# Layer 1's gate modulation: products and sums on VectorE instead of matmuls on TensorE

## The reference

```python
sc, scc = silu(c), silu(c_ctx)
for l in range(2):
    shift, scale, gate = split(sc @ w_ada[l] + b_ada[l], 3)        # w_ada[l]: 2048 x 6144
    shift_c, scale_c, gate_c = split(scc @ w_ada[l] + b_ada[l], 3)
    h = rms(x, norm_w[l]) * (1 + scale) + shift
    ...
    x = x + gate * merge_out(o_a, o_b, o_c, z, w_out[l])
    if not last:
        xc = xc + gate_c * merge_out(oa_c, ob_c, oc_c, z_c, w_out[l])
```

## Time and profile before

| | us |
|---|---|
| median of 3 runs | 3337.48 |
| lowest, highest | 3337.32, 3339.63 |
| the profiled execution | 3336.91 |
| its span, first to last instruction | 3335.1 |
| TensorE busy | 3297.0 |
| VectorE busy | 2125.5 |
| ScalarE busy | 1413.5 |
| POOL busy | 596.1 |

### The profile page before, as it was taken

One profiled execution on the slowest core, in us unless ns is written; L12 is line 12 of the kernel. 1 busy time (PEld: TensorE's weight loads), 2 busy tenths in 40 slices (PEclk: granted clock), 3 DMA queues, 4 the chain that ended last, 5 costly groups with the idle time before them and its releaser, 6 DMA issues.

```text
span 3335.1 us, 57286 instructions
## 1 busy us (share of the span) xinstructions
PE 3297.0 (99%) x21136; PEld 2818.5 (85%) x21136; DVE 2125.5 (64%) x3139; ACT 1413.5 (42%) x2160; POOL 596.1 (18%) x531
## 2 busy tenths in 40 slices
PE   8999999999999999999999999999999999999999
PEld 8999999989888888788987787778877788888978
DVE  7887877567776666767664556634553375764665
ACT  5444445544433343454532423532342263544353
POOL 4999920111440000000300000000001100000000
PEclk9999999999999999999999999999999999999999
DMA  6555555564677877777732222121235443422225
GB/s 221 183 179 184 187 185 184 185 211 165 243 266 263 278 264 272 264 260 269 249 101 98 73 88 75 54 82 63 94 108 202 145 152 108 134 94 95 95 96 181
DMA packets 158866, 554.58 MB, mean 166 GB/s; under 512 B 17456, under 2 KB 23728, under 8 KB 158640
## 3 DMA queue, kind: packets, MB, share of 16 engines
q1 hardware_dynamic: 154144, 534.67, 47.3%
q0 software_dynamic: 4496, 16.78, 1.5%
HBM read 545.09 MB, written 6.29 MB: 165 GB/s over the span
## 4 chain that ended last, share of the span: by engine, by line
PE 92%; DVE 4%; ACT 2%; DVEq 1%; issue 1%; DMA 0%; ACTq 0%; POOL 0%; SPq 0%
PE psum L2012 19%; PE psum L2014 18%; PE psum L2013 18%; PE psum L2037 14%; PE psum L2038 7%; PE psum L2066 3%; PE psum L2342 2%; PE psum L2368 2%; PE psum L2353 2%; DVE wlo L1253 1%; PE psum L2138 1%; PE psum L2299 1%; ACT whi L798 0%; PE psum L2228 0%; ACTq L869 0%
## 5 line engine op out<-in xcount | busy, mean ns | idle before, releaser
L1253 DVE TENSOR_TENSOR wlo<-raw,whi 128x1024 fp32r<-128x1024 f32 (+3 forms) x844 | 1033.6, 1230 | 570.0 <-ACT whi L798 541.2
L798 ACT ACTIVATE whi<-raw 128x1024 fp32r<-128x1024 f32 (+3 forms) x844 | 864.9, 1030 | 1058.0 <-PE psum L2014 632.9
L2012 PE MATMUL psum<-hcat,whi 128*128 128x256 f32 (+1 forms) x3436 | 1133.7, 330 | 4.7 <-DVE wlo L1253 4.0
L2014 PE MATMUL psum<-hcat,wlo 128*128 128x256 f32 (+1 forms) x3436 | 1109.7, 323 | 0.0
L2013 PE MATMUL psum<-hcat,whi 128*128 128x256 f32 (+1 forms) x3436 | 1109.3, 323 | 0.0
L2012 PEld LDWEIGHTS psum<-hcat,whi 128*128 128x128 f32 x3436 | 653.1, 190 | 90.0 <-issue 34.7
L2037 PE MATMUL psum<-hcat,whi 128*128 128x512 f32 x2048 | 727.4, 399 | 0.1
L2013 PEld LDWEIGHTS psum<-hcat,whi 128*128 128x128 f32 x3436 | 653.6, 190 | 52.0 <-issue 3.8
L2014 PEld LDWEIGHTS psum<-hcat,wlo 128*128 128x128 f32 x3436 | 653.1, 190 | 51.5
L2038 PE MATMUL psum<-hcat,wlo 128*128 128x256 f32 x2048 | 573.7, 280 | 0.0
L2037 PEld LDWEIGHTS psum<-hcat,whi 128*128 128x128 f32 x2048 | 384.5, 188 | 114.4 <-issue 25.6
(11 more groups left out here) (260 smaller groups left out, 3499.5 us busy)
## 6 DMA issues: line engine op xcount, KB each, us to landing
raw<-in_stream SPq DMA_DIRECT2D x978, 512.0 KB, 3.8
raw<-in_stream SPq DMA_DIRECT2D x18, 384.0 KB, 3.0
raw<-in_stream SPq DMA_DIRECT2D x24, 256.0 KB, 2.6
resid_dram<-X POOLq DMA_DIRECT2D x2, 2048.0 KB, 8.6
bias<-in_natten POOLq DMA_DIRECT2D x16, 256.0 KB, 2.9
X<-resid_dram POOLq DMA_DIRECT2D x4, 1024.0 KB, 6.2
raw<-in_stream SPq DMA_DIRECT2D x16, 192.0 KB, 2.5
X<-in_xT SPq DMA_DIRECT2D x4, 512.0 KB, 7.1
```

The lines of the kernel that those rows point to most:

```text
L798: act.activation(whi[:, c % HI_SLOTS, 0:n], raw[:, slot, 0:n], ACT.Copy).then_inc(hi_ready, 1)
L1253: vec.tensor_tensor(wlo[:, slot, 0:n], raw[:, slot, 0:n], whi[:, c % HI_SLOTS, 0:n].bitcast(F32), ALU.subtract).then_inc(lo_ready, 1)
L2012: pe.matmul(dst, h, cat[:, kk, c0:c0 + width], start=(q == 0 and k == 0), stop=False)
L2014: last = pe.matmul(dst, l_, cat[:, kk, c0:c0 + width], start=False, stop=(q == nq - 1 and k == nch - 1))
```

## The change

Stage out0 no longer multiplies w_ada's quarters on TensorE. The host lays out layer 1's last third in another way: output features on the partitions, and the 2048 numbers of a feature's column along the row, two quarters of 1024 for 128 features. POOL stores silu(c) into DRAM (`c_dram`) after the square sums of w_o, and loads it back as one row of 2048 repeated on all partitions (`crow`) after layer 0's values are transposed. For each quarter VectorE multiplies it with its half of `crow` and adds up along the row, starting from `b_ada` or from the sum of the first half (`tensor_tensor_reduce`), behind a `fence` (a drain). Only c is done; c_ctx's gate of layer 1 isn't computed.

The list changes to none in T0 and T1, three in T2 to T7, two in T8 to T14, none in T15. The products of tile t stand on VectorE between its two subtractions. TensorE frees the quarters, together with the tile's own last one, at the tile's last matmul, and before that matmul it waits for the products (`gate_mods`).

```diff
--- before.py
+++ after.py
@@ -116,7 +116,7 @@
 Z_CONV = [[[4], [5, 6]], [[], [], [7, 8], [9, 10]]]
 
 Z_PAIRS = 4
-MOD_OUT = [0] + [4] * 4 + [2] * 8 + [0] * 3
+MOD_OUT = [0] * 2 + [3] * 6 + [2] * 7 + [0]
 Z_WEAVE = [weave([2] * Z_SPLIT[0][0], [0] * KD), weave([2] * Z_SPLIT[1][0], [0] * KD, Z_BEFORE)]
 OUT_WEAVE = weave([2] * KD, MOD_OUT)
 FFN_BLOCKS = sum(MOD_FFN) // 8
@@ -247,6 +247,7 @@
 
 
 def build(nc, stream, xT, ctxT, params, consts, natten, out):
+    c_dram = nc.dram_tensor("c_dram", (P * KD,), F32, kind="Internal").ap()
     resid = nc.dram_tensor("resid_dram", (P, KD * 2 * S), F32, kind="Internal").ap()
 
 
@@ -271,6 +272,7 @@
     region("consts", CO["invcount"] * 4)
     region("small", (96 * 2 + KD * 35 + 24 + LAYERS * H_B + S + 120) * 4)
     region("work", 16 * KIB)
+    region("gate_mod", 2 * KD * 4)
     raw = sb("raw", [SLOTS, QW], F32, "raw")
     wlo = sb("wlo", [SLOTS, QW], F32R, "raw")
     whi = sb("whi", [HI_SLOTS, QW], F32R, "whi")
@@ -312,6 +314,11 @@
     racc = sb("racc", [2, 2 * S], F32, "q", 20 * KIB)
     scaled = sb("scaled", [2, 2, S], F32, "q", 24 * KIB)
     hfull = sb("hfull", [2, 2, S], F32, "q", 28 * KIB)
+
+    crow = sb("crow", [2 * QW], F32, "q", 0)
+    row_product = sb("row_product", [2, QW], F32, "q", 8 * KIB)
+    c_silu = sb("c_silu", [KD], F32, "gate_mod", 0)
+    gate_half = sb("gate_half", [KD], F32, "gate_mod", KD * 4)
 
     ln_sum = sb("ln_sum", [2, S], F32, "q", 20 * KIB)
     up = sb("up", [S], F32, "work", 6 * KIB)
@@ -393,6 +400,9 @@
         ln_act = sem("ln_act")
         acc_hi = sem("acc_hi")
         c_sig = sem("c_sig")
+        c_stored = sem("c_stored")
+        crow_in = sem("crow_in")
+        gate_mods = sem("gate_mods")
         rows_ready = sem("rows_ready")
         fold_ready = sem("fold_ready")
         rope_in = sem("rope_in")
@@ -1629,6 +1639,7 @@
             cvec = pv("cvec", 0, 2 * KD).rearrange("p (k c) -> p k c", c=2)
             vec.memset(cs[:, :, 2:], 0.0)
             vec.tensor_tensor(cs[:, :, 0:2], cvec, csig[:, :, :], ALU.mult)
+            vec.tensor_tensor(c_silu[:, :], cvec[:, :, 0], csig[:, :, 0], ALU.mult)
             vec.tensor_scalar(sinks[:, :], pv("sink", 0, LAYERS * H_B), -1.0, None, ALU.mult)
             vec.tensor_tensor(fin_gain[:, :], pv("final_g", 0, KD), pv("final_g", 0, KD), ALU.mult)
             fence()
@@ -1967,6 +1978,18 @@
                                                         gate_col(c, 48 * l + 2 * KD + j), xj, ALU.mult, ALU.add)
                     last.then_inc(psum_free, 1)
 
+                def row_products(e):
+
+                    for pos, a in e["mods"]:
+                        s, (t, half_) = Q0["out0"] + pos, divmod(a, 2)
+                        j = 48 + 2 * KD + t
+                        start = gate_half[:, t:t + 1] if half_ else pv("b_ada", j)
+                        total = ada_t[:, 0, j:j + 1] if half_ else gate_half[:, t:t + 1]
+                        vec.wait_ge(raw_in[s % SLOTS], 16 * (s // SLOTS + 1))
+                        fence()
+                        vec.tensor_tensor_reduce(row_product[:, a % 2, :], raw[:, s % SLOTS, :], crow[:, QW * half_:QW * half_ + QW],
+                                                 1.0, start, ALU.mult, ALU.add, total).then_inc(gate_mods, 1)
+
                 def out_tiles(i):
                     for k in range(8):
                         lo(C0["out1"] + k + AHEAD, 8 * i)
@@ -1981,14 +2004,15 @@
                     out_tiles(3)
                 else:
                     gains(1)
+                    vec.wait_ge(crow_in, 16)
                     for t, e in enumerate(OUT_WEAVE):
-                        for k in range(2 if t < KD - 1 else 1):
-                            lo(C0["out0"] + 2 * t + k + AHEAD)
+                        lo(C0["out0"] + 2 * t + AHEAD)
+                        row_products(e)
+                        if t < KD - 1:
+                            lo(C0["out0"] + 2 * t + 1 + AHEAD)
                         s = Q0["out0"] + e["pos"] + 1
                         out_tile(0, t, BANK[T0["out0"] + t], s, 0)
                         vec.drain().then_inc(x_tile, 1)
-                        mod_add(e, OUT_BLOCK)
-                        mod_rows(e, s, 0)
 
 
         @block.tensor
@@ -1997,7 +2021,7 @@
 
                 return whi[:, c % HI_SLOTS, col:col + n], wlo[:, SQ[c] % SLOTS, col:col + n]
 
-            def tile(s, d, ts, td, cat, c0, loff, width, nq=2, nch=8, k0=0, ready=None, beside_=None):
+            def tile(s, d, ts, td, cat, c0, loff, width, nq=2, nch=8, k0=0, ready=None, beside_=None, rows=()):
 
 
                 pe.wait_ge(psum_free, FREE[ts] + td)
@@ -2011,10 +2035,12 @@
                         h, l_ = weight(s + q, P * k)
                         pe.matmul(dst, h, cat[:, kk, c0:c0 + width], start=(q == 0 and k == 0), stop=False)
                         pe.matmul(dst, h, cat[:, kk, c0 + loff:c0 + loff + width], start=False, stop=False)
+                        if rows and q == nq - 1 and k == nch - 1:
+                            pe.wait_ge(gate_mods, rows[-1][1] + 1)
                         last = pe.matmul(dst, l_, cat[:, kk, c0:c0 + width], start=False,
                                          stop=(q == nq - 1 and k == nch - 1))
                         if k == nch - 1:
-                            last.then_inc(weights_used, 1)
+                            last.then_inc(weights_used, 1 + (len(rows) if q == nq - 1 else 0))
                         if beside_ and k % 4 == 3:
                             beside_(2 * q + k // 4)
 
@@ -2496,11 +2522,10 @@
                     if t < 2:
                         out_chunks(l, t, Y_EARLY, KD)
                     elif t < KD - 1:
-                        tile(C0["out0"] + e["cpos"], 0, T0["out0"] + t, 0, hcat, 0, 2 * S, w, k0=Y_PLACE)
+                        tile(C0["out0"] + e["cpos"], 0, T0["out0"] + t, 0, hcat, 0, 2 * S, w, k0=Y_PLACE,
+                             rows=e["mods"])
                     else:
                         last_out0(0).then_inc(half_done, 1)
-                    mod_fold(e, OUT_BLOCK)
-                    mod_quarters(e["mods"], Q0["out0"], 0)
 
 
         @block.gpsimd
@@ -2580,6 +2605,8 @@
             pool.drain()
             repeat(pool, 4, wo)
             pool.drain().then_inc(sq_ready, 1)
+            pool.wait_ge(vector_stage, STAGE["silu_c"])
+            pool.dma_start(c_dram.rearrange("(p k) -> p k", p=P), c_silu[:, :]).then_inc(c_stored, 16)
             for c in range(FF_REST):
                 piece(PIECE["ffn"] + c, 0, thirdcat, c, 0, S)
             for k in range(KD):
@@ -2632,6 +2659,10 @@
                 pool.dma_start(r, X[:, :, 0:S]).then_inc(spilled, 16)
                 pool.wait_ge(vt_used, VTS_OF[f"a{l}"][1] + 1)
                 biases_in(f"a{l}")
+                if l == 0:
+                    pool.wait_ge(c_stored, 16)
+                    pool.wait_ge(vt_used, VTS_OF["c0"][-1] + 1)
+                    pool.dma_start(crow[:, :], c_dram.unsqueeze(0).to_broadcast([P, P * KD])).then_inc(crow_in, 16)
                 for a, b, done in ((0, 8, 4), (8, KD, len(YCAT))):
                     pool.wait_ge(ycat_lo, len(YCAT) * l + done)
                     pool.dma_start(X[:, a:b, 0:S], r[:, a:b, :]).then_inc(resid_in[a // 8], 16)
@@ -2673,6 +2704,8 @@
     put(_quarters(w["w_o"][0]))
     up = _quarters(w["ffn_up"][0])
     ada = w["w_ada_2"].reshape(LAYERS, 8, 2, P, 12, 512).transpose(0, 4, 1, 3, 2, 5).reshape(-1, P, QW)
+    rows = w["w_ada_2"][1][:, 2 * D:].reshape(KD, P, KD, P).transpose(2, 3, 1, 0).reshape(KD, P, 2, QW)
+    ada = np.concatenate([ada[:8 * OUT_BLOCK], rows.transpose(0, 2, 1, 3).reshape(-1, P, QW)])
 
     def put_woven(weave_, tiles_, mod0):
```

## The result

The changed kernel takes 3354.81 us (median of 5 runs, 3354.51 to 3357.09) against 3338.23 (5 runs, 3337.32 to 3339.63): a ratio of 1.0053, 95% interval 1.0042 to 1.0064. It is 16.6 us slower, where 20 us of matmuls were taken off TensorE. The forecast was 3352.5, in a range of 3338 to 3365.

A forecast was written before the change was run, and what follows sets the result against it. TensorE, busy 3297.0 of 3335.1 us, bounds the kernel; its new wait closes a chain without slack. Stage 177.9 against 162.35, +15.55, plus 0.2 outside, on 3336.9: 3352.6, stated as 3352.5; range 3338 to 3365.

The forecast's parts named there:

- tile's end to landing of T(t+2).q0: From a tile's last matmul: 0.15 us to issue, 4.8 until the first weight quarter two tiles on has landed.
- landing to end of q1's subtraction: From that first weight quarter's landing through copies, addition and square to the end of the second quarter's subtraction: 6.93 us.
- signal and last matmul: At a tile's end, from the products' completion through TensorE's last matmul: 0.5 us.
- period of T3 to T7: Five output tiles with three w_ada quarters: 16.6 us from end to end against 10.95 of matmuls, TensorE stalling 5.7.
- T2, T8: Edge output tiles, first with three w_ada quarters and first with two: 13.5 and 14.0 us.
- T9 to T14 with the clock's 1.7: Six later output tiles with two w_ada quarters: no stall, 65.7 us, plus 1.7 for a lowered TensorE clock.
- the ring: In out0, closed chain between tile ends through release, load, copy, subtractions, addition, square, products and last matmul: 16.6 us.
- Slack after all: In out0, products finish before the matmuls end, all 20.0 us are kept: 3317 us; chance 0.13.
- Half of it: In out0, some chain legs overlap, seven tiles stall some 3.3 us each: 3340 us; chance 0.11.
- Half speed: VectorE's product takes 2.3 us instead of 1.3 for 1024 elements: +38.5, 3375 us; chance 0.06.
- Clock staying low: TensorE runs whole tiles at 1.2 GHz behind a stall, six tiles at +5.3: 3384 us; chance 0.03.
- The price of the sum: VectorE's writing out of each product's sum: between nothing and ScalarE's 0.20 us, taken as 0.10.

The follow-up runs named there:

- the versions without a wait: Changed kernel with all products first, then both subtractions, then the addition: 3315.75 us; changed kernel with two w_ada quarters a tile: 3318.05 us.
- The first four experiments: Changed kernel with: products, both subtractions, then addition, 3315.75 us; products alone moved ahead, 3342.92; products of 8 elements, 3336.79; two w_ada quarters a tile, 3318.05.
- the extra matmuls: Changed kernel with 16 unread matmuls on TensorE before its wait in five three-quarter tiles: 3357.54 us, ratio 1.0056.
- the one with the added work outside: Kernel before plus the silu(c) multiply, its store, the crow load and VectorE's wait for it, modulation left on TensorE: 3337.48 us, ratio 0.9999.

## Why the prediction held, point by point

| step | predicted | measured |
|---|---|---|
| matmuls removed | 20.0 | 20.7 (161.96 - 141.27, the versions without a wait) |
| outside the stage | +0.2 | 0 within 0.1% |
| product, start to start | 1.41 | 1.42 |
| tile's end to landing of T(t+2).q0 | 4.95 | 5.7 (4.85 to 6.31) |
| landing to end of q1's subtraction | 6.93 | 6.93 in each of the five turns |
| three products | 4.23 | 4.26 |
| signal and last matmul | 0.5 | 0.86 |
| period of T3 to T7 | 16.6 | 17.7 |
| T2, T8 | 13.5, 14.0 | 14.4, 13.8 |
| T9 to T14 with the clock's 1.7 | 67.4 | 65.3 |
| stage | +15.55 | +20.0 (181.92 - 161.96) |

**The mechanism** is the one forecast: the new wait closes a ring over release, load, copy, subtraction, addition, square and products, in the tiles with three w_ada quarters and not in those with two (T8, which follows one with three, waits 0.49). The first four experiments show it: a better order alone, or leaving out the fifth quarter alone, removes all waits, and products of 8 elements leave half of them.

**Mis-sized: the landing.** The forecast took one burst of before, 4.3 us from the second issue. After the change it is 4.1 to 5.6 in the five turns, 4.9 on average. The second load is issued 0.7 after the tile's end (2537.3 - 2536.57), as forecast, and once 1.1. Over five periods that is 0.72 x 5 = 3.6 us. Why the second load lands later in some turns no run here shows.

**Mis-sized: signal and last matmul.** The forecast had 0.5 for both. From the product's last row to the matmul go 0.15 (2553.56 + 0.08 to 2553.79), and the matmul takes 0.76 in four of the five turns and 0.47 in one. The long ones follow waits of 3.89 to 5.79, but so does the short one, at T4 (4.73); so the wait alone doesn't decide it. Five times 0.36 is 1.8 us.

**Misplaced: the clock.** The 1.7 us were charged to T9. The windows show 0.76 at 2587 to 2601, mostly T8, and 1.00 from 2601 on. In T8 it takes the room of the stall: the tile waits 0.49 where 2 to 3 were forecast. From T9 on the tiles take 65.3, the 1.7 and 0.07 a tile less than forecast. Within the ring TensorE idled for 4.8 and not 5.7 of a period of 17.7, since its matmuls took 13 us at the lower clock; as forecast, that was hidden, and the extra matmuls bear it out.

**The reading of before.** T15 starts at 2651.51 and not at 2651.83, which is its third matmul, and TensorE did wait once with modulation behind the tiles, 0.50 at 2529.05 for a fold. The stage of before is thus 161.96 and not 162.35.

**The sum.** In the profiled executions the stage grows by 20.0, 4.4 more than forecast, and the whole by 3355.86 - 3336.91 = 18.95. The difference is outside the stage: the changed kernel ends T1 2.4 us ahead (2487.15 against 2489.55) and takes 1.4 longer from T15 on. The forecast has no term for either. The medians differ by 16.6: the profiled execution of the changed kernel lies 1.05 over its median, that of before 1.3 under the median of the shared runs. So the forecast's 3352.5 comes within 2.3 of the median of 3354.8 in part by luck: the stage was forecast 4.4 too short, and the lead less what is lost behind it took 1.0 off that, the place of the median another 1.05.

**The rivals.** Slack after all (0.13) falls, and was nearer than it looked: it needed the chain 5.7 shorter, and another order of the same instructions does more than that. Half of it: falls for the change as it is. Half speed falls: 1.284 us for 1024 elements with two float32 sources in SBUF, against 1.23 for the plain subtraction. The half throughput that the Trainium skill, "Vector Engine (DVE) Microarchitecture Reference", section "Points that are easy to get wrong", states for an operation of this family is not seen in this one. Clock staying low for a whole tile falls: behind T2's wait the matmuls were 0.23 apart again from 2505.96, and T9 ran at 1.00. The price of the sum was put between 0 and 0.20; it is 0.08, in an instruction of its own, as the Trainium skill, "VectorE: DVE Perf Modes", section "Two Vector instructions with no wait between them", has it, at less than half of ScalarE's price.

## What to carry to other kernels

Before work is moved to an engine with idle time, follow the buffer that the new wait holds back until the wait comes round again, and compare the length of that ring with the period; the engine's busy share says nothing on it. If the ring is too long, look for an order in which the new work doesn't stand behind this turn's load: here the same products cost 16.6 us in one order and gained 22.6 in another, while moving them alone, without the conversions, ended 0.1% over the kernel before. And a chain that is shortened may bring two instructions together that slow each other.

## What was not expected of the hardware

- A product of 128x1024 float32 with its sum is two instructions on VectorE: 1.284 us and 0.08, 1.42 from one start to the next with a fence between.
- Beside POOL's addition of 128x512 the same product takes 2.07 to 2.10, and POOL's addition mostly 1.60 to 1.81 instead of 1.29. A subtraction of 1.47 may be the same thing in small: the one at 2547.91 in the changed kernel starts while POOL adds (2547.00 + 1.29). That is not shown; no run took POOL's addition away there alone.
- The time at which out0 begins differs by 2.7 us between the kernel before and the one with the added work outside, and what follows out0 took 3.0 us longer in the latter; in the changed kernel the two are 2.4 and 1.4. No run shows the cause of either.
